# Laying x and the first QKV slab out as one array of four pieces, and adding both token halves up as they land

## What is computed

```python
def rms_norm(x, g):
    xf = x.astype(jnp.float32)
    y = xf * lax.rsqrt(jnp.mean(xf * xf, axis=-1, keepdims=True) + EPS)
    return (y * g.astype(jnp.float32)).astype(x.dtype)

def mixer_a(h, w_qkv, q_gain, k_gain, w_o, cos, sin):
    B, S, _ = h.shape
    qkv = (h @ w_qkv).reshape(B, S, A_GROUPS, 3, A_HEADS, HEAD_DIM)
    ...
        q = partial_rope(rms_norm(qkv[:, :, g, 0], q_gain[g]), cos, sin)
        k = partial_rope(rms_norm(qkv[:, :, g, 1], k_gain[g]), cos, sin)
        v = qkv[:, :, g, 2]
```

## Time and profile before

| | before |
|---|---|
| median of 3 runs | 2239.18 us (2237.79 to 2241.25) |
| span of the profiled execution | 2238.0 us |
| TensorE matmul busy | 2136.5 us (95%) |
| VectorE busy | 876.9 us (39%) |
| ScalarE busy | 343.1 us (15%) |
| mean granted clock | 0.988 |
| DMA | 623.22 MB, mean 278 GB/s |

### The profile page before, as it was taken

The page is one execution under the profiler, slowest core; times in us unless marked ns, Lnnn a source line. Parts: engine busy times, 40 slices in busy tenths (PEclk is TensorE's granted clock), DMA queues, the critical chain, the costliest instruction groups (busy, mean ns, idle before and its releaser), DMA issues.

```text
span 2238.0 us, 25518 instructions
## 1 busy us (share of the span) xinstructions
PE 2136.5 (95%) x10046; PEld 1348.7 (60%) x10046; DVE 876.9 (39%) x1937; ACT 343.1 (15%) x657; POOL 21.5 (1%) x28
## 2 busy tenths in 40 slices
PE   9999999999999999999999989888999999889888
PEld 5666668888888888757644443343657554333333
DVE  3444433455331455465443222222355643222222
ACT  1222221000000000224111101010323111100110
POOL 0000000000000000000000000000000000000000
PEclk9999999999999999999999999999999999999999
DMA  7333346787445686423399999999632599999996
GB/s 312 113 130 125 132 151 241 264 303 267 142 151 221 254 309 246 143 102 132 157 369 411 429 429 428 429 428 417 236 122 76 229 401 421 428 429 428 429 428 279
DMA packets 108582, 623.22 MB, mean 278 GB/s; under 512 B 6096, under 2 KB 8528, under 8 KB 73424
## 3 DMA queue, kind: packets, MB, share of 16 engines
q1 hardware_dynamic: 94816, 566.63, 63.0%
q0 software_dynamic: 12672, 50.33, 6.1%
q10 hardware_dynamic: 1008, 5.07, 0.6%
HBM read 620.96 MB, written 1.05 MB: 278 GB/s over the span
## 4 chain that ended last, share of the span: by engine, by line
PE 76%; DMA 19%; DVE 2%; issue 1%; ACT 1%; SPq 0%; DVEq 0%; ACTq 0%
DMA ring<-in_w_up 18%; PE ps L1922 15%; PE ps L2480 14%; PE ps L1997 11%; PE ps L1959 10%; PE ps L2163 5%; PE ps L2514 4%; PE ps L2156 3%; PE ps L2313 2%; PE ps L2452 2%; PE ps L2493 1%; PE ps L2050 1%; PE ps L2020 1%; PE ps L2040 1%; PE ps L2030 1%
## 5 line engine op out<-in xcount | busy, mean ns | idle before, releaser
L2480 PE MATMUL ps<-ring,hT 128*64 128x512 f32 x1984 | 460.8, 619 | 67.9 <-DMA ring<-in_w_up 52.5
L2480 PEld LDWEIGHTS ps<-ring,hT 128*64 128x64 f32 x1984 | 166.7, 142 | 352.1 <-issue 345.6
L1922 PE MATMUL ps<-hT,ring 128*128 128x256 f32 x1408 | 309.8, 381 | 3.6 <-ACT tmp L690 2.4
L1922 PEld LDWEIGHTS ps<-hT,ring 128*128 128x128 f32 x1408 | 267.9, 191 | 41.9 <-issue 3.1
L1997 PE MATMUL ps<-ring,hT 128*128 128x384 f32 x768 | 256.4, 487 | 1.9 <-DMA ring<-in_a_wqkv 1.8
L2514 PE MATMUL ps<-ring,arena 128*64 128x512 f32 x1024 | 226.8, 595 | 1.4 <-ACT arena L995 1.4
L1959 PE MATMUL ps<-arena,ring 128*128 128x256 f32 x1024 | 224.5, 378 | 0.0
L1959 PEld LDWEIGHTS ps<-arena,ring 128*128 128x128 f32 x1024 | 193.3, 189 | 28.1
L1997 PEld LDWEIGHTS ps<-ring,hT 128*128 128x128 f32 x768 | 142.2, 190 | 93.2 <-DMA ring<-in_a_wqkv 2.5
L2514 PEld LDWEIGHTS ps<-ring,arena 128*64 128x64 f32 x1024 | 70.6, 137 | 139.8 <-issue 138.0
L1219 DVE SCALAR_TENSOR_TENSOR arena<-arena,small 128x512 f32<-128x512 f32 x168 | 126.4, 752 | 6.0
(11 more groups left out here) (380 smaller groups left out, 1756.6 us busy)
## 6 DMA issues: line engine op xcount, KB each, us to landing
ring<-in_w_gate SPq DMA_DIRECT2D x44, 2048.0 KB, 17.1
ring<-in_w_up SPq DMA_DIRECT2D x44, 2048.0 KB, 17.3
ring<-in_w_down SPq DMA_DIRECT2D x44, 2048.0 KB, 15.9
ring<-in_mlp_w SPq DMA_DIRECT2D x32, 2048.0 KB, 8.0
arena<-in_w_mod POOLq DMA_DIRECT2D x24, 2048.0 KB, 9.7
ring<-in_w_up SPq DMA_DIRECT2D x40, 1024.0 KB, 9.0
ring<-in_w_down SPq DMA_DIRECT2D x40, 1024.0 KB, 8.9
ring<-in_a_wqkv SPq DMA_DIRECT2D x24, 1536.0 KB, 6.8
```

Of the source, the lines that this page charges most:

```text
L1922: e = te.matmul(out[:, j, :], w[:, k, c0 + 128 * j:c0 + 128 * j + 128], src[:, k, :], start=(k == order[0]), stop=(k == order[-1]))
L2480: e = te.matmul(bank(b)[SB * h:SB * h + SB], xg[:, P * k + SB * h:P * k + SB * h + SB], slabs.tile(n + h).rearrange("p (k n) -> p k n", k= ...
```

## The change

The host now builds `x_by_residue` as four pieces side by side. Piece p holds, for the two contraction tiles `HEAD_ORDER[2p]` and `HEAD_ORDER[2p+1]` (0, 2 / 4, 6 / 1, 3 / 5, 7), x (512 values a partition) and then slab 0's columns (768 values). The four pieces go to the end of the arena, not to the ring: slot 0 stays empty in the first round and SyncE counts it as landed. The two table transfers move from SyncE's list to the head of ScalarE's. TensorE computes both token halves of slab 0 in `project_first`, piece by piece, then `sums_first`, then `project(0, 2)`.

```diff
-        sp.dma_start(common[:, :], common_d).then_inc(consts_in, 16)
-        sp.dma_start(param_1[:, :], param_1_d).then_inc(consts_in, 16)
         if first:
             for p in range(4):
-                sp.dma_start(xp[:, 2 * p:2 * p + 2, :].rearrange("p k t -> p (k t)"),
-                             xp_d[:, 512 * p:512 * p + 512]).then_inc(xp_in[p], 16)
+                sp.dma_start(head_in[p], xp_d[:, HEAD_PIECE * p:HEAD_PIECE * p + HEAD_PIECE]).then_inc(xp_in[p], 16)
...
                     n = A_QKV + 3 * c + w
-                    load(n, ring.tile(n)[:, 0:KD * WIDTH_A], a_wqkv[c, w])
                     if n == A_QKV:
-                        ring.wait_landed(sp, n)
+                        sp.wait_ge(xp_in[3], 16)
+                        sp.sem_inc(landed[n % SLOTS], 16)
+                    else:
+                        load(n, ring.tile(n)[:, 0:KD * WIDTH_A], a_wqkv[c, w])
...
         own = Steps(act, act_step)
+        act.dma_start(param_1[:, :], param_1_d).then_inc(consts_in, 16)
+        act.dma_start(common[:, :], common_d).then_inc(consts_in, 16)
...
                 act.wait_ge(xp_in[p], 16)
-                sc.activation(tmp[:, 512 * p:512 * p + 512], xp[:, 2 * p:2 * p + 2, :].rearrange("p k t -> p (k t)"),
-                              ACT.Square).then_inc(x_squared, 1)
-            ring.wait_landed(act, A_QKV)
+                k = HEAD_ORDER[2 * p]
+                sc.activation(tmp.rearrange("p (k t) -> p k t", k=KD)[:, k:k + 3:2, :], head_x[p], ACT.Square
+                              ).then_inc(x_squared, 1)
             act.dma_start(const_a[:, :], const_a_d).then_inc(const_a_in, 16)
...
-            for k in range(KD):
-                if k % 2 == 0:
-                    dve.wait_ge(xp_in[k // 2], 16)
-                e = ve.tensor_scalar(h3[:, k, :], xp[:, k, :], par1("norm1")[:, k:k + 1], None, ALU.mult)
-                if k % 2:
-                    e.then_inc(h_ready, 1)
+            for p in range(4):
+                dve.wait_ge(xp_in[p], 16)
+                for m, k in enumerate(HEAD_ORDER[2 * p:2 * p + 2]):
+                    e = ve.tensor_scalar(h3[:, k, :], head_x[p][:, m, :], par1("norm1")[:, k:k + 1], None, ALU.mult)
+                e.then_inc(h_ready, 1)
...
             for k in range(KD):
-                if k % 2 == 0:
-                    pe.wait_ge(x_squared, k // 2 + 1)
+                if k == 0:
+                    pe.wait_ge(x_squared, 4)
...
+            def project_first():
+
+                for p in range(4):
+                    pe.wait_ge(h_ready, p + 1)
+                    for r in range(NT):
+                        for m, k in enumerate(HEAD_ORDER[2 * p:2 * p + 2]):
+                            e = te.matmul(bank(r)[:, 0:WIDTH_A], h3[:, k, r * P:(r + 1) * P], head_w[p][:, m, :],
+                                          start=(p == 0 and m == 0), stop=(p == 3 and m == 1))
+                        if p == 3:
+                            e.then_inc(slab_done if r else half_done, 1)
...
                 before = c > 0
-                project(c, 0)
                 if before:
+                    project(c, 0)
                     turn_q(c - 1, 3)
+                    project(c, 1)
                 else:
+                    project_first()
                     sums_first(7)
-                project(c, 1)
```

More of the change, by code:

```diff
@@ L259, in program @@
     oT = take(KD * S).rearrange("p (k t) -> p k t", k=KD)
-    xp = oT
+    HEAD_PIECE = 2 * S + 2 * WIDTH_A
+    head_in = [arena[:, ARENA - 96 - (4 - p) * HEAD_PIECE:ARENA - 96 - (3 - p) * HEAD_PIECE] for p in range(4)]
+    head_x = [a[:, 0:2 * S].rearrange("p (k t) -> p k t", k=2) for a in head_in]
+    head_w = [a[:, 2 * S:HEAD_PIECE].rearrange("p (k n) -> p k n", k=2) for a in head_in]
     ca_c, ca_n = columns(CONST_A)
@@ L1994, in project @@
                 for k in HEAD_ORDER:
-                    if n == 0 and k % 2 == 0:
-                        pe.wait_ge(h_ready, k // 2 + 1)
                     e = te.matmul(bank(r)[:, 0:WIDTH_A], h3[:, k, r * P:(r + 1) * P], weights[:, k, :],
@@ L2711 @@
     feature_major = lambda a: a.T.reshape(KD, P, S).transpose(1, 0, 2).reshape(P, -1)
+    x_first = feature_major(x[order]).reshape(P, KD, S)
+    w_first = i["a_wqkv"][0].reshape(KD, P, GROUPS_A, 3, KD, P).transpose(4, 3, 1, 0, 2, 5)[0, 0].reshape(P, KD, WIDTH_A)
+    head = np.concatenate([a[:, HEAD_ORDER[2 * p:2 * p + 2], :].reshape(P, -1) for p in range(4) for a in (x_first, w_first)], 1)
     arrays = {
-        "x_t": feature_major(x), "x_by_residue": feature_major(x[order]),
+        "x_t": feature_major(x), "x_by_residue": head,
         "common": np.concatenate([common, by_partition(i["c_2"][0])], 1), "const_a": const_a, "const_2": const_2,
```

## The result

| | before | changed |
|---|---|---|
| median | 2239.39 us (6 runs, 2237.79 to 2241.25) | 2247.23 us (6 runs, 2245.0 to 2249.5) |
| ratio to before | | 1.0036, 95% interval 1.0025 to 1.0048 |
| span of the profiled execution | 2238.0 us | 2245.6 us |
| mean granted clock | 0.988 | 0.985 |

The change makes the kernel slower by 0.36%, 7.8 us between the medians. Timed again beside the experiments, the ratio was 1.0028 (1.0018 to 1.0039). The forecast was 2243.0 in a range of 2239 to 2247: the median lies just above the range.

What follows compares the result with a forecast made beforehand. TensorE, busy for 95% of the span, was taken as the bound. Stall -1.79, tables +1.2, fill -0.3, bubble +2.95 and clock +1.8 gave +3.9 us: span 2241.9, median 2243.0, range 2239.0 to 2247.0.

Steps and rivals of the forecast that it cites:

- The path: Start of TensorE's chain: a shift of the moment 26.97, when project(0, 2) starts, goes through to the end one for one.
- The stall removed: TensorE's wait for slab 0 after its fill matmuls: the whole stall goes, -1.79 us.
- The tables: Landing of common, which the fill waits for: shares the DMA engines with the head, lands at 4.7, +1.2 us.
- rival C: TensorE's first wait: common lands late and tables become the bound; landing at 7 gives +6.2 us, 2245.4; chance 0.22.
- The fill: TensorE's fill matmuls at the start: unchanged work, less time at the low clock, -0.3 us (-1.3 to +0.4).
- The bubble: TensorE idle between sums and project(0, 2), waiting for VectorE's chain up to the gain product: 3.0 us, +2.95 net.
- The clock: TensorE's granted clock around project(0, 2): falls after one-column sums with idle time behind them, +1.8 us (0 to 3.0).
- Rival B: TensorE's clock holds through the idle time behind the sums: +2.1 us, 2241.3; chance 0.19.
- The sum: All terms at the start together: +3.9 us, 2241.9 for the profiled span and 2243.0 for the median.
- Within 0.2%: Whole kernel: time differs by less than 4.5 us, taken as indistinguishable from no change; chance 0.61.
- The upper end of the range: Whole kernel: 2247.0 us, with the tables landing at 7 and a long low stretch of the clock.

Runs made afterwards that it cites:

- tables_sp: The changed kernel with both table transfers back at the head of SyncE's list; median 2242.3 us, ratio 1.0011 to the kernel before.
- one_table: The changed kernel with param_1 appended to common, one table transfer in place of two, same bytes; 2248.61 us, ratio 1.0047; repeated, 2247.11 us, ratio 1.0030.
- sums_late: The kernel before with only the one-column sums moved behind project(0, 1); median 2245.8 us, ratio 1.0025.
- after_2: The changed kernel profiled and timed again without an edit; 2247.25 us, ratio 1.0028 to the kernel before.
- sums_early: The changed kernel with the one-column sums moved ahead of piece 2 of the first projection; median 2243.7 us, ratio 1.0023 to the kernel before.
- both: The changed kernel with tables at the head of SyncE's list and sums ahead of piece 2; median 2238.6 us, ratio 0.9990 to the kernel before.
- tables_act: The kernel before with only the two table transfers moved to the head of ScalarE's queue; median 2240.0 us, ratio 1.0005.
- fill_gap: The changed kernel with four fill matmuls, results unread, put behind the sums in the idle time; median 2244.4 us, ratio 1.0020 to the kernel before.
- spread: The changed kernel with tables on SyncE's list, three fill matmuls not six, sums in portions, xT issued behind slab 1; 2236.4 us, ratio 0.9984 to the kernel before.
- spread6: The changed kernel with only tables on SyncE's list and sums in portions (six fill matmuls, xT behind slab 2); ratio 0.9997 to the kernel before.

## Why the prediction was wrong, step by step

**The path.** Right: the shift of project(0, 2) goes through. The start holds 7.48 of the 7.6 us between the spans, though that the rest is so small is luck, as +2.7 and -2.6 cancel behind it.

**The stall removed.** Right: -1.79, and the projection followed the fill at once. The head was in by 10.37 (ScalarE's last square), inside the forecast's 10 to 11.

**The tables: the step that failed.** The term "tables" was put at +1.2 us, from const_a's "133 KB/us", and the traces have +4.13. The step priced common by its bytes and gave param_1, 28 KB, no cost at all. In the changed kernel's trace the two queues took turns packet by packet instead. At 8 rows a table on each of the 16 engines and 0.19 us for a 5 KB row, an estimate, common's rows wait 1.5 us where the forecast had 1.1, and param_1's wait another 1.5 where it had none. That is 3.1 of the 4.13; the other 1.0 no run prices (in the trace the first 5 KB packets took up to 1.2 us each, and it isn't shown that they are the reason). `tables_sp` gives the whole 4.13 back; `one_table` gives 1.47 back for param_1's turns, with the same bytes. This was rival C: a landing at 7 was priced there, with a chance of 0.22 and with "only two pieces can be in front at 1.17" against it. What was in front was not whole pieces but a turn for every packet. The quoted rule of the Trainium skill was right, that the queues interleave on the same engines; the +1.2 that I hung on it was my own sizing.

**The fill.** -0.26 against -0.3.

**The bubble.** Right in place, releaser and size: 3.0 forecast, 3.31 measured. It stood at 3.32 in every profile with the sums behind both halves and nothing put into the gap (`tables_sp`, `sums_late`, `one_table` twice, `after_2`).

**The clock.** +1.8 forecast, +2.53 measured, inside the bounds of 0 to 3.0. The reason given, that the idle time behind the sums is needed for it, fell: in `sums_early`, `both` and `tables_act` the clock fell within the 32 one-column matmuls, and in `fill_gap` just behind them, with no idle time. `tables_act` has the order of the kernel before, so the 1.00 over the sums in the earlier trace rows was no fixed property of that order. How much of the 2.53 is the change's one profile of the kernel before can't say, but the runs can: the mean granted clock over the 14 runs of the changed kernel was 0.9854, over the 87 runs of the kernel before beside the experiments 0.9868. The difference of 0.0014 is some 6 us more at half speed in a run, so about 3 us lost, an estimate. So most of the term looks like the change's. Rival B, by the Trainium skill's TensorE: Matmul & The Clock Gate, section "HAM oscillation", named idle gaps alone; these traces show falls without any.

**The sum.** 3.9 forecast and 7.5 measured at the start: 2.9 of the missing 3.6 are the tables, 0.7 the clock, 0.3 the bubble, less 0.4 of faster projection, whose cause no run looked at; the other terms make up 0.1. At the tables' true +4.13 the same sum gives +6.8 and 2246.

**The chances.** "Within 0.2%" had 0.61 and slower 0.36; slower came. With tables and clock uncertain by 3 us each on one side, a sum of +3.9 under a bound of 4.5 was too near it for 0.61. The upper end of the range, 2247.0, was itself rounded up: its terms, 6.2 and 1.2 us, give 2246.6.

## What to carry to other kernels

When a small load goes out beside large ones on another queue, count its packets and price each at one packet of the neighbour, as the least that it costs: this gave 3.1 of 4.1 us beside 5 KB rows and 1.6 of 2.9 beside 2 KB rows (`tables_act`). When work is reordered, look for the dependent chain that the moved piece used to cover, here 2.3 us of small VectorE instructions under a projection. And before an engine is made earlier, look up which wait was satisfied only just in time, here ScalarE's for slab 2.

## What the runs showed of the hardware

Packets of two queues went out nearly one for one (119 to 126, then 95 to 87), with rows of 5 KB against rows of 0.2 and 1.7 KB; beside rows of 2 KB (`tables_act`) it was 186 to 80 in one window. TensorE's granted clock went to 0.50 during 3.5 us of one-column matmuls, or just behind them, with TensorE busy throughout, in four profiles (`sums_early`, `both`, `tables_act`, `fill_gap`), and stayed at 1.00 over them in the earlier trace rows. With the same sums in portions of 8 and 16 between full matmuls the clock stood at 1.00 over them in both profiles (`spread`, `spread6`); in `spread6` it fell later, behind 2.66 us of idle time.
